# Prompt attention of a hybrid decoder step: scores from 64-row halves with strided queries, mask added in PSUM, a new order of the turns

## The chip, the cores and the metric

The kernel runs on one core of one Trainium2 chip, as one launch. The metric is the device time of the launch in microseconds (us), the median of several runs. A measurement of this kernel can tell a difference of about 0.2% (6.5 us) from none.

## What is computed

One inference step of one decoder layer, for a prompt of 1024 tokens and 32 sample tokens (8 sequences of 4) with shared weights, model width 1024. Per layer: RMS norm, one input projection, an RWKV-7 branch (16 heads of 64), a dilated sliding-window attention branch, gates and an output projection, a squared-ReLU MLP, a gated embedding, and a final norm. The change touches only the attention of the prompt:

```python
def dilated_attn_prompt(q, k, v, dilation, n_back):
    ...
    qb = to_blocks(q)
    kb = with_prev(to_blocks(k))
    vb = with_prev(to_blocks(v))
    s = jnp.einsum('ndbqhe,ndbkhe->ndbhqk', qb, kb) * ATTN_SCALE
    ...
    s = jnp.where(mask[None, None, :, None], s, NEG)
    m = jnp.max(s, axis=-1, keepdims=True)
    e = jnp.exp(s - m)
    den = jnp.sum(e, axis=-1, keepdims=True)
    o = jnp.einsum('ndbhqk,ndbkhe->ndbqhe', e / den, vb)
    lse = (m + jnp.log(den))[..., 0].transpose(0, 1, 2, 4, 3)
```

There are three groups of four heads with head width 64. Their windows and dilations are (128, 1), (512, 4) and (2048, 16). Everything is float32.

## The kernel before, in words

The program goes through its stages one after another; each is a block in which the five engines run their own instruction lists and meet at its end. For each group g of 0, 1, 2 there are three blocks: the projection of q, k and v (`attention_projection`), the prompt's attention (`attention_prompt`), and the scores of the sample tokens (`sample_scores`). Then `attention_ends` reads back what the prompt's attention has stored in DRAM and weights the groups. The RWKV pairs, the merge, the MLP and the rest follow.

`qT` and `kT` hold queries and keys with features on the partitions: two heads share a tile of 128 rows, head 0 in rows 0 to 63 and head 1 in rows 64 to 127. `attention_prompt` takes 8 turns per group, one per 128 queries. A turn has 128 or 256 keys: in group 0 256 from turn 1 on, in group 1 128 in even turns and 256 in odd ones, in group 2 always 128. In groups 1 and 2 the tokens of a turn lie 4 and 8 elements apart in `qT` and `kT`.

A turn t of the kernel before is this:

- GpSimd copies the queries of each head into its row half of `qz` (L419). VectorE has set `qz` to zero at the block's start (L467), so the other half of each 128-row stationary operand is zero.
- TensorE multiplies them with the keys, four matmuls into the PSUM tile `S[t % 2]` (L440). S has two buffers.
- VectorE adds the mask and writes the result to `sc` in SBUF (L474), then takes the negated maximum per row into `stage` (L477). `stage` has two buffers.
- ScalarE takes four exponentials, one per head, with the row sums as a second output, into `ex` (L496).
- TensorE transposes `ex` into PSUM `PT` (L449), ScalarE copies it to `pt` (L498), TensorE multiplies with the values into PSUM `O` (L457).
- VectorE copies O into `stage` (L481) and SyncE stores `stage` to `attention_rows` in DRAM (L514).

The order on each engine is written out: on TensorE `scores(t+1)`, then `rest(t)` (transposes and values of t); on VectorE `maxima(t+1)` (mask and maximum), then `values(t)` (the copy of O); on ScalarE the four exponentials of t, then the copy of t. The maximum of turn t waits for the landed store of turn t-2, which read the same half of `stage`:

```python
vec.wait_ge(stored[s], (k + g * (NB // 2)) * 16)
vec_s.done("max", nc.vector.tensor_reduce(stage[:, s, AW:AW + HPG], ...
```

At the start of each `attention_prompt` ScalarE also issues the prefetch DMAs for later blocks (L489). The turns run in hardware loops of two turns (`turns` and `turns_ahead`, loops at L364, L369 and L383), with register arithmetic for addresses and semaphore values.

Of the kernel before, what the change touches and what calls it, by code (L numbers as in the profile page):

```python
# [17 lines left out]
P = 128  # L18
# [313 lines left out]
def prompt_counts(nc, top):  # L332

    sem = lambda n: top.enter_context(nc.semaphore(f"att_{n}"))
    names = {"pool": ["q0", "q1"], "score": ["scores"], "pe": ["pt", "pv"], "vec": ["mask", "max"], "out": ["o"], "act": ["e0", "e1", "e2", "e3", "pt"]}
    return [Steps(sem(n), names[n], ahead=2) for n in names], sem("zero"), [sem(f"stored{s}") for s in range(2)]


def attention_prompt(nc, top, g, counts, psum, qT, kT, vtok, att, ident, scratch, prefetch):

    with ExitStack() as ctx:
        sb = lambda n, *s: ctx.enter_context(nc.sbuf_tensor(f"{n}{g}", [P, *s], F32))
        qz, stage = sb("qz", 2, 2, 2, BL), sb("stage", 2, STG)
        sc, ex, pt = sb("sc", HPG, 2 * BL), sb("ex", HPG, 2 * BL), sb("pt", HPG, 2, BL)
# [3 lines left out]
        (pool_s, score_s, pe_s, vec_s, out_s, act_s), zero, stored = counts  # L351
# [3 lines left out]
        def turns(eng, unit):  # L355

            def run(t, half_t, parity):
                first = half_t if g == 1 else t
                both = {0: not (isinstance(t, int) and t == 0), 1: parity == 1, 2: False}[g]
                unit(t, first, both, parity, half_t)  # L360

            if g == 0:
                run(0, 0, 0)
                with eng.Fori(0, NB // 2 - 1) as i:  # L364
                    run(2 * i + 1, i, 1)
                    run(2 * i + 2, i + 1, 0)
                run(NB - 1, NB // 2 - 1, 1)
            else:
                with eng.Fori(0, NB // 2) as i:  # L369
                    run(2 * i, i, 0)  # L370
                    run(2 * i + 1, i, 1)

        def turns_ahead(eng, first_part, rest):

            def run(part, t, half_t, parity):
                both = {0: not (isinstance(t, int) and t == 0), 1: parity == 1, 2: False}[g]
                part(t, half_t if g == 1 else t, both, parity, half_t)

            run(first_part, 0, 0, 0)
            if g == 0:  # L380
                run(first_part, 1, 0, 1)
                run(rest, 0, 0, 0)
                with eng.Fori(0, NB // 2 - 1) as i:  # L383
                    run(first_part, 2 * i + 2, i + 1, 0)
                    run(rest, 2 * i + 1, i, 1)
                    run(first_part, 2 * i + 3, i + 1, 1)
                    run(rest, 2 * i + 2, i + 1, 0)
            else:
                with eng.Fori(0, NB // 2 - 1) as i:
                    run(first_part, 2 * i + 1, i, 1)  # L390
                    run(rest, 2 * i, i, 0)
                    run(first_part, 2 * i + 2, i + 1, 0)
                    run(rest, 2 * i + 1, i, 1)
                run(first_part, NB - 1, NB // 2 - 1, 1)
                run(rest, NB - 2, NB // 2 - 1, 0)
            run(rest, NB - 1, NB // 2 - 1, 1)

        with nc.Block() as block:
            @block.gpsimd
            def _(pool):  # L400
                if g == 0:
                    pool_s.begin(pool)
                pool.wait_ge(zero, g + 1)

                def unit(t, f, both, s, k):
                    score_s.wait(pool, "scores", t - 2)
                    for h in range(2):
                        rows = slice(h * HD, (h + 1) * HD)
                        src = qT[rows, :, 0:SEQ]
                        if g == 0:  # L410
                            src = src[:, :, bass.ds(f * BL, BL)]
                            dst = qz[rows, s, :, h, :]
                        elif g == 1:
                            src = src.rearrange("p a (i r) -> p a r i", r=STEP[1])[:, :, bass.ds(f, 1), (BL if both else 0):(2 * BL if both else BL)].rearrange("p a o i -> p a (o i)")
                            dst = qz[rows, s, :, h, :]
                        else:
                            src = src.rearrange("p a (i r) -> p a r i", r=STEP[2])[:, :, bass.ds(f, 1), :].rearrange("p a o i -> p a (o i)")
                            dst = qz[rows, s, :, h, :]
                        pool_s.done(f"q{h}", nc.gpsimd.tensor_copy(dst, src))  # L419
                turns(pool, unit)  # L420

            @block.tensor
            def _(pe):
                if g == 0:
                    pe_s.begin(pe)
                if g == 0:
                    score_s.begin(pe)

                def scores(t, f, both, s, k):
                    nk = 2 * BL if both else BL  # L430
                    pool_s.wait(pe, "q1", t)
                    vec_s.wait(pe, "mask", t - 2)
                    for h in range(HPG):
                        if g == 0:
                            keys = dilated(kT[:, h // 2, 0:SEQ], 0, f - 1 if both else f, nk)
                        elif g == 1:
                            keys = dilated(kT[:, h // 2, 0:SEQ], 1, f, nk, 0)
                        else:
                            keys = dilated(kT[:, h // 2, 0:SEQ], 2, f, nk)
                        last = nc.tensor.matmul(S[s][:, h, 0:nk], qz[:, s, h // 2, h % 2, :], keys, start=True, stop=True)  # L440
                    score_s.done("scores", last)

                def rest(t, f, both, s, k):
                    nk = 2 * BL if both else BL
                    act_s.wait(pe, "e3", t)
                    act_s.wait(pe, "pt", t - 1)
                    for h in range(HPG):
                        for b in range(nk // BL):
                            last = nc.tensor.transpose(PT[:, h, b, :], ex[:, h, b * BL:(b + 1) * BL], ident)  # L449
                    pe_s.done("pt", last)  # L450
                    act_s.wait(pe, "pt", t)
                    out_s.wait(pe, "o", t - 1)
                    for h in range(HPG):
                        for b in range(nk // BL):
                            blk = (t - 1 + b) if both else t
                            v = vtok[:, bass.ds(blk, 1), h * HD:(h + 1) * HD].rearrange("p o c -> p (o c)")
                            last = nc.tensor.matmul(O[:, h * HD:(h + 1) * HD], pt[:, h, b, :], v, start=b == 0, stop=b == nk // BL - 1)  # L457
                    pe_s.done("pv", last)
                turns_ahead(pe, scores, rest)

            @block.vector
            def _(vec):
                if g == 0:
                    vec_s.begin(vec)
                if g == 0:
                    out_s.begin(vec)
                nc.vector.memset(qz[:, :, :, :, :], 0.0).then_inc(zero, 1)  # L467

                def maxima(t, f, both, s, k):
                    nk = 2 * BL if both else BL  # L470
# [6 lines left out]
                    vec_s.done("max", nc.vector.tensor_reduce(stage[:, s, AW:AW + HPG], sc[:, :, 0:nk], AXX, ALU.max, negate=True))  # L477

                def values(t, f, both, s, k):
                    pe_s.wait(vec, "pv", t)  # L480
                    out_s.done("o", nc.vector.tensor_copy(stage[:, s, 0:AW], O))  # L481
                turns_ahead(vec, maxima, values)

            @block.scalar
            def _(act):
                if g == 0:
                    act_s.begin(act)
                for dst, src, loaded in prefetch:
                    act.dma_start(dst, src).then_inc(loaded, 16)  # L489

                def unit(t, f, both, s, k):
                    nk = 2 * BL if both else BL
                    vec_s.wait(act, "max", t)
                    pe_s.wait(act, "pt", t - 1)
                    for h in range(HPG):
                        act_s.done(f"e{h}", nc.scalar.activation(ex[:, h, 0:nk], sc[:, h, 0:nk], ACT.Exp, bias=stage[:, s, AW + h:AW + h + 1], accum_out=stage[:, s, AW + HPG + h:AW + HPG + h + 1]))  # L496
                    pe_s.wait(act, "pt", t)
# [1923 lines left out]
```

## Time and profile before

| | |
|---|---|
| median of 3 runs | 3240.7 us (3236.83 to 3241.89) |
| the profiled execution: its own time | 3243.15 us |
| its span | 3241.3 us |
| PE (TensorE) busy | 2892.0 us, 89% of the span |
| DVE (VectorE) busy | 1093.4 us, 34% |
| ACT (ScalarE) busy | 954.7 us, 29% |
| POOL (GpSimd) busy | 408.0 us, 13% |
| the three prompt-attention blocks | about 145 to 209, 313 to 387 and 491 to 550 us of the span |

PE is the matrix engine's matmuls, PEld its weight loads, SPq and ACTq the queues that issue DMAs. A float32 matmul appears as two records. PEclk is the granted TensorE clock as a share of 2.4 GHz; 0.50 means 1.2 GHz all the time.

### The profile page before, as it was taken

The page shows a single profiled execution, that of the slowest core. Times are in us where ns is not written, and L with a number is a line of the kernel's source. Part 1 is how long each engine was busy: PE and PEld are TensorE (multiplying, and loading weights), DVE is VectorE, ACT ScalarE, POOL GpSimd, SP SyncE. Part 2 cuts the span into 40 slices and gives each one's busy share as a digit, 9 for nine tenths or more (in the row PEclk, how much of TensorE's full clock was granted, in tenths as well). Part 3 has the DMA queues.
Part 4 walks back from the last instruction along what each step waited for, and adds up shares of the span by engine and source line. Part 5 has one row for each costly group of instructions (what it writes and reads, how often), then busy time and mean ns, then how long its engine had stood idle before and what let it go on. Part 6 is the DMA issues. An engine that isn't in the chain of part 4 may idle for free. (4 is left out here: it accounts for less than half of the span.)

```text
span 3241.3 us, 62579 instructions
## 1 busy us (share of the span) xinstructions
PE 2892.0 (89%) x27170; PEld 2307.8 (71%) x27170; DVE 1093.4 (34%) x2436; ACT 954.7 (29%) x1797; POOL 408.0 (13%) x398
## 2 busy tenths in 40 slices
PE   5888795699999999999978999898999999999797
PEld 3666575356666666666665666597999999999685
DVE  1120202247777777777760101103111111111222
ACT  1120202145555555555541000003122211122212
POOL 0000001011111111211100000011121212121010
PEclk8989796799999999999978999999999999999898
DMA  3211104200100100101001001111111111111011
GB/s 138 80 64 60 71 14 148 65 22 3 34 25 11 34 19 17 34 3 33 13 2 69 29 34 42 39 66 39 39 45 39 45 39 39 45 39 45 30 41 62
DMA packets 57762, 139.16 MB, mean 43 GB/s; under 512 B 5041, under 2 KB 37041, under 8 KB 52433
## 3 DMA queue, kind: packets, MB, share of 16 engines
q1 hardware_dynamic: 53376, 112.89, 10.3%
q10 hardware_dynamic: 4176, 23.20, 2.1%
q8 instruction: 166, 2.72, 0.3%
q14 instruction: 44, 0.35, 0.0%
HBM read 119.54 MB, written 16.54 MB: 42 GB/s over the span
## 5 line engine op out<-in xcount | busy, mean ns | idle before, releaser
L1557 PE MATMUL psum<-hT,rkv_w 128*64 128x256 f32 (+1 forms) x3072 | 411.9, 395 | 11.5 <-DMA rkv_w<-in_w_pair 10.2
L1557 PEld LDWEIGHTS psum<-hT,rkv_w 128*64 128x64 f32 x3072 | 212.6, 138 | 116.0 <-issue 31.4
L129 PE MATMUL psum<-hT,merge_w 128*128 128x352 f32 x768 | 232.4, 463 | 12.1 <-DMA merge_w<-in_w_mix 12.1
L1878 POOL TENSOR_TENSOR ff_w_low<-ff_raw,ff_w_high 128x1024 fp32r<-128x1024 f32 x64 | 157.3, 2457 | 677.8 <-ACT ff_w_high L1873 677.8
L129 PEld LDWEIGHTS psum<-hT,merge_w 128*128 128x128 f32 x768 | 147.1, 192 | 95.2 <-issue 15.0
L152 PE MATMUL psum<-ff_high,ff_w_high 128*128 128x352 f32 x768 | 173.2, 335 | 38.7 <-DVE ff_low L2177 38.7
L2180 DVE TENSOR_TENSOR rwkv_out<-rwkv_out,psum 128x1056 f32<-128x1056 f32 x64 | 80.3, 1254 | 321.1 <-PE psum L152 321.1
L152 PE MATMUL psum<-h_high,ff_w_high 128*128 128x352 f32 x768 | 167.6, 326 | 13.0 <-DVE h_low L226 12.6
L152 PE MATMUL psum<-ff_low,ff_w_high 128*128 128x352 f32 x768 | 170.3, 331 | 0.0
L152 PE MATMUL psum<-ff_high,ff_w_low 128*128 128x352 f32 x768 | 169.9, 330 | 0.0
L1873 ACT ACTIVATE ff_w_high<-ff_raw 128x1024 fp32r<-128x1024 f32 x64 | 67.3, 1052 | 347.5 <-PE psum L152 347.5
L152 PE MATMUL psum<-h_low,ff_w_high 128*128 128x352 f32 x768 | 166.2, 325 | 0.0
L152 PE MATMUL psum<-h_high,ff_w_low 128*128 128x352 f32 x768 | 166.2, 324 | 0.0
L152 PEld LDWEIGHTS psum<-ff_high,ff_w_high 128*128 128x128 f32 x768 | 136.0, 197 | 41.0 <-issue 41.0
L2177 DVE TENSOR_TENSOR ff_low<-ff_up,ff_high 128x1056 fp32r<-128x1056 f32 x32 | 40.3, 1258 | 351.4 <-ACT ff_high L2162 351.4
L129 PE MATMUL psum<-hT,w_qk 128*128 128x352 f32 x432 | 130.9, 466 | 22.6 <-DMA w_qk<-in_w_qk 21.3
L152 PEld LDWEIGHTS psum<-h_high,ff_w_high 128*128 128x128 f32 x768 | 131.3, 190 | 15.0 <-issue 10.8
L152 PEld LDWEIGHTS psum<-ff_high,ff_w_low 128*128 128x128 f32 x768 | 135.9, 194 | 0.0
L152 PEld LDWEIGHTS psum<-ff_low,ff_w_high 128*128 128x128 f32 x768 | 135.5, 195 | 0.0
L1997 DVE TENSOR_TENSOR merge_prod<-merge_gate,psum 128x1056 f32<-128x1056 f32 x16 | 20.1, 1255 | 335.7 <-PE psum L129 335.7
L129 PEld LDWEIGHTS psum<-hT,w_qk 128*128 128x128 f32 x432 | 83.1, 193 | 69.9 <-DMA w_qk<-in_w_qk 21.8
L152 PEld LDWEIGHTS psum<-h_high,ff_w_low 128*128 128x128 f32 x768 | 132.6, 189 | 0.0
(323 smaller groups left out, 5209.0 us busy)
## 6 DMA issues: line engine op xcount, KB each, us to landing
ff_raw<-in_w_ff SPq DMA_DIRECT2D x64, 512.0 KB, 3.5
merge_w<-in_w_mix SPq DMA_DIRECT2D x8, 1664.0 KB, 6.9
rkv_w<-in_w_pair SPq DMA_DIRECT2D x24, 512.0 KB, 4.1
rwkv_out<-in_kc ACTq DMA_DIRECT2D x4, 2048.0 KB, 13.1
ple_w<-in_w_ple SPq DMA_DIRECT2D x8, 640.0 KB, 3.9
x_in<-in_xT SPq DMA_DIRECT2D x2, 2112.0 KB, 11.1
rwkv_out<-in_xT ACTq DMA_DIRECT2D x1, 4224.0 KB, 14.1
out_yT<-y SPq DMA_DIRECT2D x8, 528.0 KB, 3.1
```

What stands on the lines that cost most here:

```text
L129: last = nc.tensor.matmul(acc[:, n, 0:TT], w[:, k, :], x[:, k, n * TT:(n + 1) * TT], start=k == 0, stop=k == kt - 1)
L152: last = nc.tensor.matmul(acc[:, n, 0:TT], a[:, k, :], b[:, k, n * TT:(n + 1) * TT], start=k == 0 and b is x_hi and a is w_hi, stop=k == k ...
L1557: mm = nc.tensor.matmul(ahead[half[a], 0:width(v)], w3[:, k, n * P + a * C:n * P + a * C + C], hT[:, k, cols(v)], start=k == 0, stop=k == ...
L1873: return nc.scalar.activation(parts[0][:, s, :], raw[:, s, 0:KT * P], ACT.Copy)
L1878: return nc.gpsimd.tensor_tensor(parts[1][:, s, :], raw[:, s, 0:KT * P], parts[0][:, s, :].bitcast(F32), ALU.subtract)
L1997: vec_s.done(f"mul{b}", nc.vector.tensor_tensor(thirds(prod[:, b, :]), thirds(gate[:, b if nb == 2 else s, :]), acc[1][:, :, 0:TT], ALU.mult))
L2177: vec_s.done(f"low{c}", nc.vector.tensor_tensor(ff[1][:, c, :], up[:, c % 2, :], ff[0][:, c, :].bitcast(F32), ALU.subtract))
L2180: vec_s.done(f"add{m}", nc.vector.tensor_tensor(thirds(x[:, m, :]), thirds(x[:, m, :]), acc[m % 2][:, :, 0:TT], ALU.add))
```

## The change

Queries are no longer copied: each head's scores are a matmul over its own 64 rows of `qT` and `kT`, with the stationary queries read in place (strided in groups 1 and 2). The four heads' scores are placed so that the heads of the upper and the lower row half write different PSUM banks (`slot`). `qz`, its memset, GpSimd's copies and `sc` are gone. The mask is added to S in place, in PSUM, and the maximum and the exponentials read PSUM. `ex` has two buffers. TensorE takes the scores of turn t+2 between the transposes and the values of turn t. ScalarE copies turn t-1's transposes between the second and the third exponential of turn t. The copy has a semaphore of its own. All turns are written out, without hardware loops.

```diff
-    names = {"pool": ["q0", "q1"], "score": ["scores"], "pe": ["pt", "pv"], "vec": ["mask", "max"], "out": ["o"], "act": ["e0", "e1", "e2", "e3", "pt"]}
+    names = {"score": ["scores"], "pe": ["pt", "pv"], "vec": ["mask", "max"], "out": ["o"], "act": ["e0", "e1", "e2", "e3"], "copy": ["pt"]}
...
-        qz, stage = sb("qz", 2, 2, 2, BL), sb("stage", 2, STG)
-        sc, ex, pt = sb("sc", HPG, 2 * BL), sb("ex", HPG, 2 * BL), sb("pt", HPG, 2, BL)
+        stage = sb("stage", 2, STG)
+        ex, pt = sb("ex", 2, HPG, 2 * BL), sb("pt", HPG, 2, BL)
...
+        slot = lambda h: 2 * (h % 2) + h // 2
+        both = lambda t: (t > 0, t % 2 == 1, False)[g]
+        keyed = lambda t: 2 * BL if both(t) else BL
...
+                def scores(t):
+                    act_s.wait(pe, "e3", t - 2)
+                    for b in range(2):
+                        for a in range(2):
+                            rows = slice(a * HD, (a + 1) * HD)
+                            last = nc.tensor.matmul(S[t % 2][:, slot(2 * b + a), 0:keyed(t)], queries(t, rows, b), keys(t, rows, b), start=True, stop=True)
+                    score_s.done("scores", last)
+
+                def turned(t):
+                    act_s.wait(pe, "e3", t)
+                    copy_s.wait(pe, "pt", t - 1)
...
+                def values(t):
+                    copy_s.wait(pe, "pt", t)
+                    out_s.wait(pe, "o", t - 1)
...
+                for t in range(2):
+                    scores(t)
+                for t in range(NB):
+                    turned(t)
+                    if t + 2 < NB:
+                        scores(t + 2)
+                    values(t)
...
-                nc.vector.memset(qz[:, :, :, :, :], 0.0).then_inc(zero, 1)
...
+                def maxima(t):
+                    s, nk = t % 2, keyed(t)
                     m = att("pairs") if g == 2 else att("band")[:, 2 * BL - nk:]
                     score_s.wait(vec, "scores", t)
-                    act_s.wait(vec, "e3", t - 1)
-                    vec_s.done("mask", nc.vector.tensor_tensor(sc[:, :, 0:nk], S[s][:, :, 0:nk], m[:, None, :].to_broadcast([P, HPG, nk]), ALU.add))
+                    vec_s.done("mask", nc.vector.tensor_tensor(S[s][:, :, 0:nk], S[s][:, :, 0:nk], m[:, None, :].to_broadcast([P, HPG, nk]), ALU.add))
                     vec_s.wait(vec, "mask", t)
-                    vec.wait_ge(stored[s], (k + g * (NB // 2)) * 16)
+                    vec.wait_ge(stored[s], (t // 2 + g * (NB // 2)) * 16)
...
+                maxima(0)
+                for t in range(NB):
+                    if t + 1 < NB:
+                        maxima(t + 1)
+                    values(t)
...
+                for t in range(NB):
                     vec_s.wait(act, "max", t)
-                    pe_s.wait(act, "pt", t - 1)
-                    for h in range(HPG):
-                        act_s.done(f"e{h}", nc.scalar.activation(ex[:, h, 0:nk], sc[:, h, 0:nk], ACT.Exp, bias=stage[:, s, AW + h:AW + h + 1], accum_out=stage[:, s, AW + HPG + h:AW + HPG + h + 1]))
-                    pe_s.wait(act, "pt", t)
-                    act_s.done("pt", nc.scalar.activation(pt[:, :, 0:nk // BL, :], PT[:, :, 0:nk // BL, :], ACT.Copy))
-                turns(act, unit)
+                    pe_s.wait(act, "pt", t - 2)
+                    for h in (0, 1):
+                        weights(t, h)
+                    if t:
+                        copied(t - 1)
+                    for h in (2, 3):
+                        weights(t, h)
+                copied(NB - 1)
```

`weights(t, h)` is the exponential of head h, and `copied(t)` the copy of turn t's transposes, which waits for the transposes of t and the values of t-1.

ScalarE in group 0, one loop body of two turns of the kernel before (`ex` is written by the exponentials, `pt` by the copy; L117 rows are waits and register arithmetic):

```order
L496 ACTIVATE ex,stage<-sc,stage 128x256 [waits att_pe]
L496 ACTIVATE ex,stage<-sc,stage 128x256 x3
L117 REGISTER_ALU
L498 ACTIVATE pt<-psum 128x1024 [waits att_pe]
L117 ISA
L496 ACTIVATE ex,stage<-sc,stage 128x256 [waits att_pe,att_vec]
L496 ACTIVATE ex,stage<-sc,stage 128x256 x3
L117 REGISTER_ALU
L498 ACTIVATE pt<-psum 128x1024 [waits att_pe]
```

The same place in the changed kernel, from the first turn on (L446 is the exponential, L451 the copy):

```order
L446 ACTIVATE ex,stage<-psum,stage 128x128 [waits att_pe,att_vec]
L446 ACTIVATE ex,stage<-psum,stage 128x128 x3
L446 ACTIVATE ex,stage<-psum,stage 128x256 [waits att_pe,att_vec]
L446 ACTIVATE ex,stage<-psum,stage 128x256
L451 ACTIVATE pt<-psum 128x4x128 [waits att_pe]
L446 ACTIVATE ex,stage<-psum,stage 128x256 x2
L446 ACTIVATE ex,stage<-psum,stage 128x256 [waits att_pe,att_vec]
L446 ACTIVATE ex,stage<-psum,stage 128x256
L451 ACTIVATE pt<-psum 128x1024 [waits att_pe]
L446 ACTIVATE ex,stage<-psum,stage 128x256 x2
```

The copy of a turn has moved behind the first two exponentials of the next turn.

TensorE in the changed kernel, group 0, turns 0 and 1 (L390 transposes, L382 scores, L400 values):

```order
L390 MATMUL psum<-cst_sb,ex 128x128 [waits att_copy,att_act]
L390 MATMUL psum<-cst_sb,ex 128x128 x3
L382 MATMUL psum<-kT,qT 128x256 [waits att_act]
L382 MATMUL psum<-kT,qT 128x256 x3
L400 MATMUL psum<-vtok,pt 128x64 [waits att_out,att_copy]
L400 MATMUL psum<-vtok,pt 128x64 x3
L390 MATMUL psum<-cst_sb,ex 128x128 [waits att_copy,att_act]
L390 MATMUL psum<-cst_sb,ex 128x128 x7
L382 MATMUL psum<-kT,qT 128x256 [waits att_act]
L382 MATMUL psum<-kT,qT 128x256 x3
L400 MATMUL psum<-vtok,pt 128x64 [waits att_out,att_copy]
L400 MATMUL psum<-vtok,pt 128x64 x7
```

Scores stand between transposes and values; before, they stood ahead of the transposes, and the values followed the transposes with only a wait between.

VectorE in the changed kernel, group 0, from turn 1's mask on (L421 mask, L424 maxima, L428 the copy of O):

```order
L421 TENSOR_TENSOR psum<-psum,att_sb 128x1024 [waits att_score]
L424 TENSOR_REDUCE stage<-psum 128x2x2 [waits att_stored1,att_vec]
L428 COPY stage<-psum 128x256 [waits att_pe]
L421 TENSOR_TENSOR psum<-psum,att_sb 128x1024 [waits att_score]
L424 TENSOR_REDUCE stage<-psum 128x2x2 [waits att_stored0,att_vec]
L428 COPY stage<-psum 128x256 [waits att_pe]
```

The order of the three is that of the kernel before. The mask no longer waits for the exponentials (att_act), since it writes no `sc`.

## Rows read from the trace of the kernel before

**Rows 1.** Busy times by stretch: from:to, us, each engine busy (instructions), clock, DMA share, GB/s
```profile
145.00:209.00 64.00, 48.02 (x244) 41.22 (x244) 22.91 (x26) 23.94 (x72) 6.48 (x17) 0.74 0.23 83
...
313.00:387.00 74.00, 49.07 (x208) 39.75 (x208) 19.32 (x25) 21.15 (x72) 10.14 (x16) 0.66 0.34 114
...
491.00:550.00 59.00, 37.03 (x160) 32.74 (x160) 15.33 (x25) 17.84 (x72) 10.23 (x16) 0.59 0.43 143
```

**Rows 2.** Timeline, group 0, one turn: start us, us, engine, instruction [idle before <-releaser]
```profile
171.57 1.95 PE L440 MATMUL psum<-kT,qz 128*128 x8
...
173.35 1.04 PE L449 MATMUL psum<-cst_sb,ex 128*128 128x128 f32 x8
173.67 1.22 DVE L474 TENSOR_TENSOR sc<-psum,att_sb 128x1024 f32<-128x1024 f32 x1 [1.47 <-PE psum L440]
...
174.43 1.02 ACT L498 ACTIVATE pt<-psum 128x1024 f32<-128x1024 f32 x1 [1.99 <-PE psum L449]
175.03 1.22 DVE L477 TENSOR_REDUCE stage<-sc 128x4 f32<-128x1024 f32 x1
...
175.69 1.99 PE L457 MATMUL psum<-vtok,pt 128*128 x16 [1.30 <-ACT pt L498]
176.28 0.51 ACT L496 ACTIVATE ex<-sc,stage 128x256 f32<-128x256 f32 x1 [0.83 <-DVE stage L477]
...
177.52 3.41 PE L440 MATMUL psum<-kT,qz 128*128 x8
...
177.72 0.42 DVE L481 COPY stage<-psum 128x256 f32<-128x256 f32 x1 [1.47 <-PE psum L457]
```

**Rows 3.** Timeline, the last turn of group 0
```profile
199.38 1.97 PE L449 MATMUL psum<-cst_sb,ex 128*128 128x128 f32 x8 [0.53 <-ACT ex L496]
...
202.46 3.67 PE L457 MATMUL psum<-vtok,pt 128*128 128x64 f32 x16 [1.11 <-ACT pt L498]
206.17 0.42 DVE L481 COPY stage<-psum 128x256 f32<-128x256 f32 x1 [6.86 <-PE psum L457]
```

**Rows 4.** Timeline, first and last copies of O, delayed maxima, values at 128 keys
```profile
155.98 0.42 DVE L481 COPY stage<-psum 128x256 f32<-128x256 f32 x1
...
160.03 1.22 DVE L477 TENSOR_REDUCE stage<-sc 128x4 f32<-128x1024 f32 x1 [0.71 <-DMA attention_rows<-stage]
...
333.10 0.42 DVE L481 COPY stage<-psum 128x256 f32<-128x256 f32 x1 [1.51 <-PE psum L457]
...
338.08 0.69 DVE L477 TENSOR_REDUCE stage<-sc 128x4 f32<-128x512 f32 x1 [2.28 <-DMA attention_rows<-stage]
...
384.07 0.42 DVE L481 COPY stage<-psum 128x256 f32<-128x256 f32 x1 [8.62 <-PE psum L457]
...
511.70 0.42 DVE L481 COPY stage<-psum 128x256 f32<-128x256 f32 x1 [2.58 <-PE psum L457]
...
516.60 0.69 DVE L477 TENSOR_REDUCE stage<-sc 128x4 f32<-128x512 f32 x1 [2.15 <-DMA attention_rows<-stage]
...
537.39 1.10 PE L457 MATMUL psum<-vtok,pt 128*128 x8 [0.87 <-ACT pt L498]
...
541.93 1.97 PE L457 MATMUL psum<-vtok,pt 128*128 128x64 f32 x8 [0.69 <-ACT pt L498]
...
547.44 0.42 DVE L481 COPY stage<-psum 128x256 f32<-128x256 f32 x1 [3.08 <-PE psum L457]
```

**Rows 5.** The 24 stores of stage to DRAM (L514), from issue to landing
```profile
DMA to landing us min/median/max: 1.7/1.7/4.3
```

**Rows 6.** Timeline, the first exponential of group 1; then all 24 copies of L498
```profile
327.33 0.40 ACT L496 ACTIVATE ex<-sc,stage 128x128 f32<-128x128 f32 x1 [51.38 <-issue]
...
L498 ACT ACTIVATE pt<-psum x24: 597/598/1025, 154.2 to 544.8; 128x512 f32<-128x512 f32 x13, 128x1024 f32<-128x1024 f32 x11
```

**Rows 7.** Timeline, the start of group 0: VectorE's memset and TensorE's first scores
```profile
145.98 0.91 DVE L467 MEMSET qz<- 128x1024 f32 x1 [4.75 <-ACTq L109]
...
147.85 2.50 PE L440 MATMUL psum<-kT,qz 128*128 128x128 f32 x9 [7.07 <-POOL qz L419]
```

More of the change, by code:

```diff
@@ L350, in attention_prompt @@
         O = psum[:, 6, 0:AW]
-        (pool_s, score_s, pe_s, vec_s, out_s, act_s), zero, stored = counts
+        (score_s, pe_s, vec_s, out_s, act_s, copy_s), stored = counts
         for each in counts[0]:
             each.first = g * NB
[L355 to L396, printed above, removed]
@@ L398, in attention_prompt @@
-        with nc.Block() as block:
[L399 to L420, printed above, removed]
@@ L425, in _ @@
                     pe_s.begin(pe)
-                if g == 0:
                     score_s.begin(pe)
[L429 to L432, printed above, removed]
-                    for h in range(HPG):
[L434 to L441, printed above, removed]
@@ L459, in _, with queries, keys @@
-                turns_ahead(pe, scores, rest)
+                def queries(t, rows, b):
+                    if g == 0:
+                        return qT[rows, b, t * BL:(t + 1) * BL]
+                    lo = BL if g == 1 and both(t) else 0
+                    return qT[rows, b, 0:SEQ].rearrange("p (i r) -> p r i", r=STEP[g])[:, first(t), lo:lo + BL]
+                def keys(t, rows, b):
+                    if g == 0:
+                        lo = t * BL - (BL if both(t) else 0)
+                        return kT[rows, b, lo:lo + keyed(t)]
+                    return kT[rows, b, 0:SEQ].rearrange("p (i r) -> p r i", r=STEP[g])[:, first(t), 0:keyed(t)]
@@ new lines, in scores @@
+                def scores(t):
[8 more added lines that the diff above has]
+                    copy_s.wait(pe, "pt", t - 1)
+                    for h in range(HPG):
+                        for b in range(keyed(t) // BL):
+                            last = nc.tensor.transpose(PT[:, h, b, :], ex[:, t % 2, h, b * BL:(b + 1) * BL], ident)
+                    pe_s.done("pt", last)
@@ new lines, in values @@
+                def values(t):
+                    copy_s.wait(pe, "pt", t)
+                    out_s.wait(pe, "o", t - 1)
+                    blocks = keyed(t) // BL
+                    for h in range(HPG):
+                        for b in range(blocks):
+                            v = vtok[:, t - blocks + 1 + b, h * HD:(h + 1) * HD]
+                            last = nc.tensor.matmul(O[:, h * HD:(h + 1) * HD], pt[:, h, b, :], v, start=b == 0, stop=b == blocks - 1)
+                    pe_s.done("pv", last)
@@ L503, in _ @@
                 rows = scratch.rearrange("(i r) c -> r i c", r=STEP[g])
-                def unit(t, f, both, s, k):
+                for t in range(NB):
                     out_s.wait(sp, "o", t)
@@ L508, in unit @@
                     if g == 0:
-                        dst = scratch[bass.ds(f * BL, BL), g * STG:(g + 1) * STG]
-                    elif g == 1:
-                        dst = rows[bass.ds(f, 1), (BL if both else 0):(2 * BL if both else BL), g * STG:(g + 1) * STG].rearrange("o i c -> (o i) c")
-                    else:
-                        dst = rows[bass.ds(f, 1), :, g * STG:(g + 1) * STG].rearrange("o i c -> (o i) c")
-                    sp.dma_start(dst, stage[:, s, :]).then_inc(stored[s], 16)
-                turns(sp, unit)
+                        dst = scratch[t * BL:(t + 1) * BL, g * STG:(g + 1) * STG]
+                    else:
+                        lo = BL if g == 1 and both(t) else 0
+                        dst = rows[first(t), lo:lo + BL, g * STG:(g + 1) * STG]
+                    sp.dma_start(dst, stage[:, t % 2, :]).then_inc(stored[t % 2], 16)
                 for s in range(2):
```

37 lines of the change are left out of this document (13 added, 24 removed).

## The prediction

> **What bounds the kernel now.** I read the stretches first, then the timeline of one turn, then who waits for whom. The change touches only the three prompt-attention blocks, about 64, 74 and 59 us of the 3241.3 us span [rows 1]; the rest keeps its instructions. TensorE is busy 75, 66 and 63% of them, at a granted clock of 0.74, 0.66 and 0.59. Between the levels 1.2 and 2.4 GHz that is 52, 68 and 82% of the time at 1.2.
>
> A turn's loop closes on TensorE [rows 2]: scores of the next turn 1.95, transposes 1.04, then the wait for ScalarE's copy of 1.02 us, values 1.99, and the next scores at 177.52, 5.95 us after the last ones. The mask, the maxima and the four exponentials run beside it. At 1.2 GHz the next scores take 3.41 us, and a group's last turn has transposes of 1.97 and values of 3.67 [rows 2, 3]. So the first group takes 50.19 us from its first to its last copy of O (155.98 to 206.17), 7.17 a turn; the second 50.97 (333.10 to 384.07), the third 35.74 (511.70 to 547.44) [rows 3, 4]. These seven intervals per group are what I recompute.
>
> One more dependence hardly shows yet. The maxima of turn t+2 go into the stage buffer that the store of turn t reads, so they wait until that store has landed, 1.7 us (median) after its issue [rows 5]. VectorE waits there only for the first store of each group (0.71, 2.28 and 2.15 us [rows 4]), when the prefetches load the DMA engines: from the end of the O copy to the start of the maxima 3.6, 4.6 and 4.5 us. Elsewhere the new scores come later than the store.
>
> **The change, part by part.**
> *The order on ScalarE decides.* Before, the copy of turn t comes ahead of the exponentials of t+1. Now it comes behind the first two of them. VectorE's order stays: maxima of t+1, O copy of t, maxima of t+2. This closes a loop with one turn per round: O copy (t) → store lands → maxima (t+2) → two exponentials (t+2) → copy of the transposes (t+1) → values (t+1) → O copy (t+1). In the kernel before, the same path runs through all four exponentials, the transposes and the copy of its own turn: two turns per round, about 10.5 us, hence covered by TensorE's loop. "Two turns ahead" doesn't help: VectorE won't touch those scores before the O copy.
>
> The round for 256 keys, from rows: store 1.85 (1.7 plus the hops), maxima 1.22, hop 0.1, two exponentials and the accumulator read 1.08, copy 1.02, hop 0.07, values 1.99, hop 0.05, O copy 0.42 [rows 2, 5]: **7.8 us with values at 2.4 GHz, 9.5 at 1.2** (3.67) [rows 3]. The mask (0.04 + 1.22) lies under the store's 1.85. For 128 keys maxima take 0.69, an exponential 0.40, the copy 0.60, values 1.10 or 1.97 [rows 4, 6]: 5.75 or 6.6. The second group alternates 128 and 256 keys: rounds of 7.06 and 6.49 at 2.4, of 8.74 and 7.36 at 1.2.
>
> *Clock.* TensorE's work per round shrinks or stays while the round grows, so I expect no less time at 1.2 GHz than now: 60, 75 and 90% in the three groups against 52, 68 and 82. Rounds: 8.8; 8.3 and 7.1; 6.5.
>
> *Sum per group*, six rounds, the late first store, and a last turn (transposes, copy, values in a row: 199.38 to 206.17 = 6.8 [rows 3]; third group 1.0 + 0.6 + 1.97 + hops = 3.8):
> first 52.8 + 1.8 + 6.8 = 61.4 against 50.2: +11.2;
> second 46.2 + 2.7 + 6.8 = 55.7 against 51.0: +4.7;
> third 39.0 + 2.6 + 3.8 = 45.4 against 35.7: +9.7.
>
> *Start.* The memset and the first query copies go: scores could begin at 145.98 instead of 147.85 in the first group [rows 7]. But the first copy of O now also waits for the maxima of turn 1. I take -1, between -1.9 and 0. In the other groups ScalarE first issues its own prefetch DMAs, and the first exponential of the second group starts only at 327.33, and what ended the idle time before it is "issue", not the maxima [rows 6]. This stays, so nothing is gained there.
>
> *Scores in row halves, strided queries.* No row shows these forms. They stand outside the new loop: per round TensorE has values, transposes and scores, at 1.2 GHz with full-price scores 3.67 + 1.97 + 3.41 = 9.05, under 9.5 [rows 2, 3]. Whether halves overlap (half the price) or strided weights cost as much again only inside that slack changes nothing: 0, with an upper bound of about +1 a round in the first group, +6. The Trainium skill, page "TensorEngine Tiling (Array Packing)", section "Theoretical Speedup", gives up to 2x for a contraction of 64 rows; by that rule alone the time would fall (rival 1). No run here shows row halves of this form.
>
> *No copies on GpSimd:* off the path after the start, 0. *Loops written out:* register instructions ahead of values go. TensorE's idle time ahead of values is 1.30 us in the written loop (copy 1.02) and 1.11 in the last turn outside it [rows 2, 3]; my hop of 0.07 has it.
>
> *Mask and maxima in PSUM.* The mask from PSUM into SBUF takes 1.22, the maxima from SBUF also 1.22 for 1024 elements [rows 2]; place makes no difference in these rows, so 0. Upper bound: maxima twice as dear, +1.2 in some 18 rounds, up to +22, which I think far. The Trainium skill ("Perfetto Trace Analysis", section "Optimizing Scalar/DVE Operations") puts an access at about 60 ns for VectorE in SBUF and 125 in PSUM, for ScalarE 93 and 51. By it, as an estimate, each round's maxima gain 0.065 and two exponentials lose 0.084: -0.4 us in all, against 0 by the rows.
>
> **Sum:** 11.2 + 4.7 + 9.7 - 1 = **+24.6 us**. The profiled execution took 3243.15 us, 1.85 more than its span, so it would take 3267.7. It lies 2.45 above the median of 3240.7; on the median's scale the forecast is **3265.3**.
>
> **Rivals.**
> 1. *TensorE's loop remains the bound (faster).* If the O copy did not hold back the next maxima, scores would fill the wait for ScalarE's copy (1.2 us a turn) and cost half (1.35 saved at mixed clocks): -2.5 a turn in the first group, -1.9 and -1.5 in the others, times 7: -41, 3200. For it: TensorE is the busiest engine, and every removed part is its work or ahead of it. Against: the written order on VectorE and ScalarE is fixed. It decides if stores and maxima need under 1 us together; rows say 1.85 + 1.22. 8%.
> 2. *Clock at 2.4 throughout.* Rounds of 7.8; 7.06 and 6.49; 5.75 give +5.2, -0.8, +5.2, less 1: +8.6, 3249. Against: the blocks before spend over half at 1.2 with denser work. With mixed cases near no change: 10%.
> 3. *Clock at 1.2 throughout.* +15.4, +6.8, +10.4, less 1: +31.6, 3272. Part of the forecast's range.
> 4. *PSUM or late stores dearer.* Maxima from PSUM or a second late store per group add 5 to 22: 3270 to 3294, of which over 3281 about 10%.
> 5. *The halves don't overlap:* hidden, the same time; not a case of its own.
>
> **How the numbers follow.** Forecast with its clock and store bounds (3250 to 3281) 72%, rival 1 8%, rival 2 10%, rival 4 beyond the range 10%. Over 0.2% (6.5 us, about what a measurement can tell) is under 3234 or over 3247. Faster 0.08, same 0.08 (the low part of rival 2 and mixed cases), slower 0.84. The range, 3246 to 3281, takes rival 2's end and leaves out rival 1 and the far part of 4.
>
> **What would show it.** Right: VectorE's maxima wait for the DMA attention_rows in nearly all turns with a predecessor (18 rather than 3), O copies 7.8 to 9.5 us apart in the first group and 5.7 to 6.6 in the third, TensorE idle for 2 to 4 us ahead of the values, waiting on ScalarE's copy; blocks of some 74, 79 and 68 us. The scores end several us before their mask starts. Wrong: O copies under 7 us apart in the first group; masks that wait on scores; a shorter block anywhere but in the second group; or a difference outside the three blocks.

## The result, and the profile after

The changed kernel takes 3270.23 us (median of 4 runs, 3266.95 to 3272.05), the one before 3238.76 us in the same comparison: a ratio of 1.0098, 95% interval 1.0083 to 1.0113, about 1% slower. The profiled executions are 3243.15 us before and 3270.32 after, spans 3241.3 and 3268.5: +27.2. The forecast was +24.6 us and 3265.3, range 3246 to 3281. In this text "the changed kernel" is the one with the whole change, "the kernel before" the one without it.

Busy times by stretch after (from:to, length, then PE, PEld, DVE, ACT, POOL busy with instructions, granted clock, DMA share, GB/s), over the three prompt-attention blocks:

```profile
145.00:222.00 77.00, 52.69 (x244) 44.31 (x244) 21.65 (x25) 22.00 (x72) 0.24 (x2) 0.57 0.19 69
326.00:402.00 76.00, 42.09 (x208) 34.61 (x208) 18.35 (x25) 19.45 (x72) 0.15 (x1) 0.57 0.33 111
508.00:574.00 66.00, 32.22 (x160) 27.26 (x158) 13.87 (x24) 16.04 (x72) 0.00 (x0) 0.50 0.38 128
```

Against [rows 1] GpSimd's work is gone and the blocks are longer. In the second and third group TensorE has less busy time than before, yet its clock is lower in all three: 0.57, 0.57 and 0.50 instead of 0.74, 0.66 and 0.59. At 0.50 the whole third block ran at 1.2 GHz.

The timeline after: one round of group 0, from one copy of O to the next; then the first and last copies of O of each group and, in group 1, two inner ones (start, length, engine, instruction, idle before and its releaser):

```profile
154.72 0.42 DVE L428 COPY stage<-psum 128x256 f32<-128x256 f32 x1 [3.88 <-PE psum L400]
...
177.05 1.92 PE L390 MATMUL psum<-cst_sb,ex 128*128 128x128 f32 x8
177.30 0.42 DVE L428 COPY stage<-psum 128x256 f32<-128x256 f32 x1 [5.74 <-PE psum L400]
177.64 1.22 DVE L421 TENSOR_TENSOR psum<-psum,att_sb 128x1024 f32<-128x1024 f32 x1
178.90 2.08 PE L382 MATMUL psum<-kT,qT 64*128 64x256 f32 x8
179.59 1.22 DVE L424 TENSOR_REDUCE stage<-psum 128x4 f32<-128x1024 f32 x1 [0.73 <-DMA attention_rows<-stage]
180.85 0.47 ACT L446 ACTIVATE ex<-psum,stage 128x256 f32<-128x256 f32 x1 [6.41 <-DVE stage L424]
...
181.77 1.02 ACT L451 ACTIVATE pt<-psum 128x1024 f32<-128x1024 f32 x1
...
182.84 2.21 PE L400 MATMUL psum<-vtok,pt 128*128 128x64 f32 x16 [1.86 <-ACT pt L451]
...
185.09 0.42 DVE L428 COPY stage<-psum 128x256 f32<-128x256 f32 x1 [4.27 <-PE psum L400]
...
219.10 0.42 DVE L428 COPY stage<-psum 128x256 f32<-128x256 f32 x1 [6.07 <-PE psum L400]
...
346.39 0.42 DVE L428 COPY stage<-psum 128x256 f32<-128x256 f32 x1 [14.29 <-PE psum L400]
...
364.89 0.42 DVE L428 COPY stage<-psum 128x256 f32<-128x256 f32 x1 [3.60 <-PE psum L400]
...
371.72 0.42 DVE L428 COPY stage<-psum 128x256 f32<-128x256 f32 x1 [3.84 <-PE psum L400]
...
399.21 0.42 DVE L428 COPY stage<-psum 128x256 f32<-128x256 f32 x1 [6.07 <-PE psum L400]
...
527.52 0.42 DVE L428 COPY stage<-psum 128x256 f32<-128x256 f32 x1 [15.77 <-PE psum L400]
...
571.90 0.42 DVE L428 COPY stage<-psum 128x256 f32<-128x256 f32 x1 [3.08 <-PE psum L400]
```

Read the round as a chain. The copy of O ends at 177.72 and its store lands; the maxima start at 179.59, 1.87 us later. They release the exponentials at 180.85; behind two of these stands ScalarE's copy at 181.77, behind it the values at 182.84, behind them the next copy of O at 185.09. A round of 7.79 us, with its values nearly all at 2.4 GHz (2.21 us; 1.99 and 3.67 at the two levels [rows 2, 3]). The mask and the scores run inside it without setting anything. It is the shortest full round of the group: its seven intervals between copies of O are 11.75, 10.83, 7.79, 8.62, 9.24, 9.66 and 6.49 us. The first two have a late store, and in four of the first six the values take 3.67 or 3.68 us, which is 1.2 GHz.

From first to last copy of O the groups take 64.38, 52.82 and 44.38 us against 50.19, 50.97 and 35.74 [rows 3, 4]: +24.7 of the 27.2 us. The first copy of O comes 1.3 us earlier than before, the stretches between the groups are 1.0 us longer, and the stretch behind the last copy of O is 2.7 us longer. That last difference lies in code that the change leaves alone, and can't be told from scatter: in the thirteen profiled executions of this study the stretch takes between 2690.1 and 2697.6 us, whatever the order of the turns.

The maxima after, what ended VectorE's idle time ahead of them, and who waited for them:

```profile
L424 DVE TENSOR_REDUCE stage<-psum x24: 691/692/1226, 147.4 to 564.3; 128x4 f32<-128x512 f32 x13, 128x4 f32<-128x1024 f32 x11
its engine sat idle before it (us, times) until:
  DMA attention_rows<-stage: 27.8, 18
who waited for it (us, times):
  ACT ex L446: 243.7, 22
```

Eighteen waits for the store instead of three, and an unchanged duration in PSUM (at most 1.226 us for 1024 elements; 1.22 in [rows 2]).

### The profile page after: what moved, and what is told of

The parts are those of the page before. It is cut to its first block and busy times, and to the rows that moved or that the text cites. A ratio compares the mean times of both kernels' runs of the same rounds, so it can differ in the third digit from the quotient of the medians.

```text
span 3268.5 us, 61980 instructions
## 1 busy us (share of the span) xinstructions
PE 2888.5 (88%) x27170; PEld 2303.5 (70%) x27170; DVE 1089.8 (33%) x2433; ACT 948.9 (29%) x1797; POOL 380.9 (12%) x350
```

## The experiments

**1. The orders and the store, one at a time.** Three kernels start from the changed one. `copy_back` puts ScalarE's copy ahead of the next turn's exponentials:

```diff
-                    for h in (0, 1):
-                        weights(t, h)
-                    if t:
-                        copied(t - 1)
-                    for h in (2, 3):
+                    for h in range(HPG):
                         weights(t, h)
-                copied(NB - 1)
+                    copied(t)
```

`four_stages` gives `stage` four buffers with a semaphore each (the exponentials, the copy of O and the store use `t % 4` too):

```diff
-        stage = sb("stage", 2, STG)
+        stage = sb("stage", 4, STG)
...
-                    vec.wait_ge(stored[s], (t // 2 + g * (NB // 2)) * 16)
+                    vec.wait_ge(stored[t % 4], (t // 4 + g * (NB // 4)) * 16)
```

`both` has the two together. What was expected:

> The changed kernel with ScalarE's copy of a turn back ahead of the next turn's exponentials. Theory (the one-turn loop through store, maxima, two exponentials, copy and values sets the rounds): without the moved copy the loop spans two turns again, rounds fall to 5.2 to 7.7 us at 256 keys and about 4.3 at 128, and the kernel takes about 3215 us, some 55 less than the changed kernel and about 25 less than the one before. Rival (the mask in PSUM, the strided queries or the written-out code cost the time): it stays within 10 us of the changed kernel, 3260 or more.

> The changed kernel with four stage buffers instead of two, so that maxima no longer wait for the store of two turns before; orders as changed. Theory: the store's share of the loop goes (27.8 us of VectorE's waits for the DMA in the changed kernel), the maxima follow the mask at once, the O copy still holds back the mask: about 3243 us, the level of the kernel before. Rival (the stores hide behind the O copy and the mask anyway, the order alone costs): under 8 us gained, 3262 or more.

> Copy back and four stage buffers together. Theory: the two loops are alternatives once the copy is back, so the second repair adds only the late first stores, 2 to 3 us per group: about 3208 us. Rival (the two add up): 55 and 27 less than the changed kernel, about 3188 us.

Measured: copy_back 3227.43 us, ratio to the kernel before 0.9963 (0.9949 to 0.9977); four_stages 3235.74, 0.9987 (0.9978 to 0.9997); both 3208.25, 0.9902 (0.9885 to 0.9918). Against the changed kernel's 3270.23 that is 43, 34 and 62 us less.

The moved copy is the largest part, as forecast, though with it back the time fell less than the 55 us expected. The loop through the store spans two turns now and still binds in part: in `copy_back` the maxima still wait for the DMA, and taking that wait away as well (`both`) gains 19 us more. Idle time of VectorE and ScalarE ahead of what reads or writes `stage`:

```profile
  issue: 103.5, 2
  PE psum L400: 90.6, 19
  DVE stage L424: 64.7, 14
  DMA attention_rows<-stage: 28.2, 18
```

So my "two alternatives" were wrong: the second repair is worth 19 us behind the first, not 2 to 3 per group. They don't add up to 77 either; together they gain 62. `four_stages` alone gained 34 us where 27 were expected. In it no maxima wait for the DMA, and the round's path has mask and maxima back to back:

```profile
170.42 0.42 DVE L428 COPY stage<-psum 128x256 f32<-128x256 f32 x1 [5.73 <-PE psum L400]
170.76 1.22 DVE L421 TENSOR_TENSOR psum<-psum,att_sb 128x1024 f32<-128x1024 f32 x1
172.02 1.23 DVE L424 TENSOR_REDUCE stage<-psum 128x4 f32<-128x1024 f32 x1
173.28 0.47 ACT L446 ACTIVATE ex<-psum,stage 128x256 f32<-128x256 f32 x1 [5.71 <-DVE stage L424]
```

The maxima start 1.18 us after the copy of O ends, instead of 1.87. The round from 170.42 to the next copy of O at 177.30 takes 6.88 us instead of 7.79 and still has the moved copy and the values in it. From first to last copy of O group 0 takes 50.17 us instead of 64.38; besides the shorter round, the late stores no longer count there, and the granted clock of its block is 0.67 instead of 0.57.

**2. The moved copy alone, in the kernel before.** `copy_moved` leaves everything as before except ScalarE's order (its turns written out, the copy with a semaphore of its own):

```diff
-                    for h in range(HPG):
-                        act_s.done(f"e{h}", ...)
-                    pe_s.wait(act, "pt", t)
-                    act_s.done("pt", ...)
+                    for h in (0, 1):
+                        weights(t, h)
+                    if t:
+                        copied(t - 1)
+                    for h in (2, 3):
+                        weights(t, h)
```

> The kernel before with one thing of the change: ScalarE copies turn t-1 between the second and third exponential of turn t (its turns written out, the other engines' loops kept). Theory: the loop closes here too, and longer, since the next scores stand behind the values on TensorE: scores 1.95 to 3.41, mask and maxima 2.5, two exponentials 1.1, copy 1.0, values 2.0 to 3.7 = 8.8 to 12 us a round at 256 keys and 5.3 to 7.3 at 128, about 50 us more than before, 3290 us. Rival (the order is harmless, the PSUM operands or row halves cost): within 7 us of the kernel before.

(The cut diff leaves out the two helpers, which are those of the changed kernel on `sc`, and the renamed semaphore.) Measured: 3296.09 us, 1.0178 (1.0161 to 1.0195), 6 us from the forecast. One round of its group 0:

```profile
191.76 3.73 PE L440 MATMUL psum<-kT,qz 128*128 x8
192.00 0.42 DVE L481 COPY stage<-psum 128x256 f32<-128x256 f32 x1 [5.88 <-PE psum L457]
...
195.62 1.23 DVE L474 TENSOR_TENSOR sc<-psum,att_sb 128x1024 f32<-128x1024 f32 x1 [3.19 <-PE psum L440]
196.88 1.22 DVE L477 TENSOR_REDUCE stage<-sc 128x4 f32<-128x1024 f32 x1
198.14 0.51 ACT L496 ACTIVATE ex<-sc,stage 128x256 f32<-128x256 f32 x1 [9.00 <-DVE stage L477]
...
199.13 1.00 ACT L502 ACTIVATE pt<-psum 128x1024 f32<-128x1024 f32 x1
...
200.19 3.67 PE L457 MATMUL psum<-vtok,pt 128*128 x16 [3.27 <-ACT pt L502]
...
203.90 0.42 DVE L481 COPY stage<-psum 128x256 f32<-128x256 f32 x1 [5.79 <-PE psum L457]
```

Every piece of the loop is in line, 11.9 us per turn. It closes through another engine than in the changed kernel: the scores of the next turn but one stand behind the values on TensorE, and the mask waits for them (3.19 us idle), not for a store. Nothing of PSUM, row halves or strides is in this kernel: ScalarE's order, written out, costs 56 us here.

**3. Is the copy's new place bad in itself?** `moved_copy_free_maxima` keeps the changed kernel's copy where it is and opens the loop elsewhere, with four stage buffers and VectorE's maxima of t+2 ahead of the copy of O of t. `maxima_free` is the same with the copy back.

```diff
                 maxima(0)
+                maxima(1)
                 for t in range(NB):
-                    if t + 1 < NB:
-                        maxima(t + 1)
+                    if t + 2 < NB:
+                        maxima(t + 2)
                     values(t)
```

> Copy back, four stage buffers, and on VectorE the mask and maxima of t+2 ahead of the O copy of t. Theory: the O copy no longer holds back the maxima, so truly two turns ahead; only the loop of exponentials, scores, mask and maxima over two turns and TensorE's own work remain: 4.0 to 4.5 us a turn at 2.4 GHz, 5 to 10 us less than with the first two repairs, about 3201 us. Rival (the delayed O copy holds up the values of the next turn): the same 3208 or more.

> The changed kernel with its moved copy kept, four stage buffers, and the maxima of t+2 ahead of the O copy of t. Theory: the moved copy costs only because it closes a loop through the O copy; with the maxima free of the O copy that loop is open, and the kernel is within 8 us of the one with the copy back (3192 us). Rival (the copy between the exponentials costs by itself, by delaying the values): 3215 us or more.

Measured: maxima_free 3191.82 us, 0.9846 (0.9830 to 0.9862); moved_copy_free_maxima 3194.39, 0.9856 (0.9839 to 0.9872). The two overlap. The fair comparison has four stage buffers on both sides: there the place of the copy is worth 27 us with the maxima held (`four_stages` 3235.74, `both` 3208.25) and nothing that can be measured with the maxima free. With two buffers and the maxima held it is 43 us. So the cost is the closed loop, not the copy between exponentials. `maxima_free` gained 16 us over `both`, more than the 5 to 10 expected.

**4. What the other parts are worth.** `old_orders` has both orders of the kernel before (copy back; TensorE's scores of t+1 ahead of the transposes of t) on the changed kernel's row halves, strided queries, PSUM mask and written-out turns, with two stage buffers.

```diff
-                for t in range(2):
-                    scores(t)
-                for t in range(NB):
-                    turned(t)
-                    if t + 2 < NB:
-                        scores(t + 2)
-                    values(t)
+                scores(0)
+                for t in range(NB):
+                    if t + 1 < NB:
+                        scores(t + 1)
+                    turned(t)
+                    values(t)
```

> The changed kernel with both orders as before: ScalarE copies a turn ahead of the next exponentials, TensorE takes the scores of t+1 ahead of the transposes of t. What is left of the change are the row halves, the mask in PSUM, the missing copies and the written-out turns. Theory: these parts are a gain once the one-turn loop is gone; the scores are on TensorE's loop again, at 1.1 to 2.1 us instead of 1.95 to 3.4, so 1 to 1.4 us less per turn of 256 keys and half of it at 128: about 3213 us. Rival (these parts cost): above the kernel before, 3245 or more.

Measured: 3234.75 us, 0.9978 (0.9966 to 0.9989). A gain, 7 us, but a quarter of what I expected. The scores did get cheaper: in group 0 the eight records of 64x256 take 2.08 us at 1.2 GHz, where those of 128*128 take 3.73 at that clock (first line of the `copy_moved` round above; the 3.41 in [rows 2] were measured at a granted clock of 0.55, partly above 1.2 GHz). But the clock went down with the work. Stretches of old_orders over the three blocks:

```profile
143.00:206.00 63.00, 45.59 (x244) 36.68 (x244) 22.56 (x25) 22.30 (x72) 0.68 (x2) 0.67 0.26 93
308.00:381.00 73.00, 47.69 (x208) 38.95 (x208) 18.87 (x25) 19.89 (x72) 0.11 (x1) 0.50 0.36 120
486.00:544.00 58.00, 33.86 (x160) 28.07 (x160) 14.35 (x25) 16.59 (x72) 0.13 (x1) 0.50 0.43 146
```

Clock 0.67, 0.50 and 0.50 against 0.74, 0.66 and 0.59 in [rows 1]: groups 1 and 2 now run wholly at 1.2 GHz. The third group shows what that costs. Its inner turns last 4.95 to 4.96 us in old_orders, each with values at 1.2 GHz (1.97 us). In the kernel before, the turns with values at 1.2 GHz (1.96 us) last 5.4 to 5.9 us, and the two with values at 2.4 GHz (1.10 us) 4.64 and 4.79. So at the same clock a turn became 0.5 to 1.0 us shorter, and the lost turns at 2.4 GHz took part of that back. Besides, the maxima wait 14.2 us for the stores here, against 5.1 before. No run holds the clock fixed, so how the missing 21 us divide between the two is not shown.

`scores_twice` issues each score matmul of the changed kernel twice (`for b in (0, 1, 0, 1)`), the second time over the same result.

> The changed kernel with the four score matmuls of each turn issued twice. Theory: the scores lie outside the loop, TensorE idles longer ahead of the values than they take; between -3 and +4 us against the changed kernel, 3267 to 3274 (less is possible only through a higher granted clock). Rival (row-half scores are on the path): 1.3 to 2.1 us more in each of 24 turns, about +40 us, 3310.

Measured: 3260.88 us, ratio to before 1.0058 (1.0041 to 1.0075), 9 us less than the changed kernel although TensorE does more, and below the 3267 to 3274 that I expected. Its stretches:

```profile
143.00:216.00 73.00, 50.02 (x308) 43.34 (x308) 21.84 (x25) 22.04 (x72) 0.43 (x2) 0.73 0.20 73
320.00:398.00 78.00, 50.76 (x272) 41.43 (x272) 18.35 (x25) 19.48 (x72) 0.15 (x1) 0.68 0.33 109
504.00:568.00 64.00, 37.81 (x218) 33.02 (x216) 13.97 (x24) 16.07 (x72) 0.00 (x0) 0.55 0.40 132
```

The clock is 0.73, 0.68 and 0.55 where the changed kernel has 0.57, 0.57 and 0.50. The scores are off the path, as claimed: with twice as many the rival's 3310 is 49 us away. And TensorE's idle time is not free here, since less of it came with a higher clock for the values, which are on the path: group 0 takes 58.70 us from first to last copy of O instead of 64.38. The 9 us are not all explained by this. Group 1 takes 2.0 us more and group 2 1.8 less, so that only 5.8 of the profiled executions' 12.3 us lie ahead of the last copy of O. The rest lies behind it, in the stretch that varies by as much from kernel to kernel (2690.1 to 2697.6 us, as above).

**5. Towards a faster kernel.** In every kernel of this study so far the first exponentials of groups 1 and 2 wait for ScalarE's own DMA issues. The start of group 1 in `both`, ScalarE's timeline:

```profile
291.93 6.50 ACTq L442 DMA_DIRECT2D rwkv_out<-in_kc  x2
298.46 7.00 ACTq L442 DMA_DIRECT2D w_qk<-in_w_qk  x1
305.49 0.45 ACTq L442 DMA_DIRECT2D w_kv<-in_w_kv  x1
306.05 0.37 ACT L446 ACTIVATE ex<-psum,stage 128x128 f32<-128x128 f32 x1 [51.41 <-issue]
```

The issue of the first 1.5 MB of weights took 7 us with two 2 MB transfers issued just ahead of it. In group 0, where those two have 0.5 MB each, it took 1.63. Why an issue takes so long is not shown: the next one, of another 1.5 MB and with more ahead of it, took 0.45. The same place in `prefetch_spread` (below), where one transfer is issued and nothing else:

```profile
290.03 0.70 ACTq L455 DMA_DIRECT2D rwkv_out<-in_kc  x1
292.86 0.37 ACT L445 ACTIVATE ex<-psum,stage 128x128 f32<-128x128 f32 x1 [40.13 <-DVE stage L424]
```

`prefetch_spread` is `both` with the issues ahead of turns 0, 2, 4 and 5:

```diff
-                for dst, src, loaded in prefetch:
-                    act.dma_start(dst, src).then_inc(loaded, 16)
+                issued = {0: 0, 2: 1, 4: 2, 5: 3}
...
                 for t in range(NB):
+                    if t in issued:
+                        dst, src, loaded = prefetch[issued[t]]
+                        act.dma_start(dst, src).then_inc(loaded, 16)
```

`all_repairs` adds VectorE's order of maxima_free. `all_scores_twice` is all_repairs with doubled scores.

> Copy back and four stage buffers, and ScalarE issues its four prefetch DMAs one by one, ahead of the exponentials of turns 0, 2, 4 and 5, instead of all at the block's start. Theory: the first exponentials of groups 1 and 2 wait 13 to 14 us for the second and third issue, which stall behind the first transfer; spread, the issues cost 0.5 us each and about 24 us go: 3184 us. Rival (an issue of these descriptors takes 6 to 7 us wherever it stands, or the data come too late for the sample scores and the next weights): no gain, 3208 or more.

> Copy back, four stage buffers, maxima ahead of the O copy, prefetches spread. Theory: the last two gains (16 and 27 us) lie in different places, the turns and the wait for the first exponential, and add up: about 3165 us. Rival (without the wait at the start the prefetches run into the turns, TensorE is slower there): 3175 or more.

> The kernel with all repairs and every score matmul issued twice. Theory (TensorE's work beyond the loop raises the granted clock, as in the run before, where doubled scores made the changed kernel 9 us faster): in groups 1 and 2, which run at 1.2 GHz, the clock rises, and the time is the same or up to 8 us less than with the repairs alone. Rival (with short turns TensorE is the bound, the scores are on its path): 0.7 to 2.1 us more a turn, 15 to 40 us more.

Measured: prefetch_spread 3181.03 us, 0.9817 (0.9800 to 0.9833), 27 less than `both`; all its issues take 0.33 to 0.70 us. all_repairs **3173.16 us**, 0.9797 (0.9780 to 0.9813): the best of the study, 68 us under the kernel before in its own comparison (3241.29) and 97 under the changed one. It missed its 3165 by 8: the free maxima are worth 8 us there, not 16. all_scores_twice 3182.79, 0.9822 (0.9806 to 0.9839): 10 us more. The clock rises here too, but now the scores are on the path: in group 1 the masks wait for them 25.9 us in 8 waits, against 17.6 in 8 in all_repairs. Neither of my two sizes was right, and the expectation took group 1 to run at 1.2 GHz, where all_repairs has 0.75. The higher clock may give back a part of the added work; it does not give back all.

Stretches of groups 1 and 2 in all_repairs:

```profile
285.00:335.00 50.00, 36.01 (x208) 29.04 (x208) 20.17 (x26) 19.56 (x72) 1.52 (x2) 0.75 0.59 190
430.00:480.00 50.00, 36.30 (x185) 29.64 (x188) 17.82 (x28) 16.15 (x72) 1.52 (x2) 0.56 0.57 190
```

The same in all_scores_twice: clock 0.93 and 0.78 instead of 0.75 and 0.56, with 6.7 and 5.4 us more of busy TensorE.

```profile
285.00:335.00 50.00, 42.71 (x268) 32.99 (x266) 18.20 (x24) 18.88 (x72) 0.00 (x0) 0.93 0.58 188
430.00:480.00 50.00, 41.71 (x255) 36.22 (x255) 14.98 (x26) 14.82 (x67) 0.00 (x0) 0.78 0.55 182
```

## Why the prediction was right

*The loop.* The step "the order on ScalarE decides" held in every link: 18 waits for the DMA, values waiting on the copy (122.5 us of TensorE's idle time), and a chain in which every piece follows the one before. The one full round with values near 2.4 GHz took 7.79 us where 7.8 was computed, the two wholly at 1.2 GHz behind the late stores 9.24 and 9.66 where 9.5 was. Runs 1 to 3 show it from three sides: undoing the copy's place, putting it into the old kernel, and opening the loop at another point.

*The sum per group* was +11.2, +4.7 and +9.7; measured +14.2, +1.9 and +8.6. That 24.7 before the start's gain came so near to 25.6 is partly luck, errors of opposite sign. Group 0: I took 60% of the time at 1.2 GHz, and at a granted clock of 0.57 it was 86%; and the first store held the maxima 4.4 us behind the copy of O instead of 3.6, the second 3.5 instead of 1.85. Group 1: I took three quarters of the values at 1.2 GHz, but a round from 364.89 to 371.72 takes 6.83 us, which only values of 256 keys at 2.4 GHz allow (7.06 by my sum). Group 2: all at 1.2 GHz, and 1.0 us under my sum over seven intervals, with exponentials a little shorter than I took them. The blocks, forecast at 74, 79 and 68 us, are about 77, 76 and 66.

*The start.* The first copy of O in group 0 comes at 154.72 instead of 155.98; about 0.9 us of that is the block's own, the rest its earlier begin. Forecast: -1.

*Mask and maxima in PSUM:* priced at 0, measured 1.22 us for the maxima as before. By the Trainium skill's page "Perfetto Trace Analysis", section "Optimizing Scalar/DVE Operations", they would, as an estimate, have been 0.065 us longer each; the maxima went from 1.22 us [rows 2] to 1.226 at most, so this trace does not show it. The other half of that estimate, exponentials 0.042 us shorter each, the trace does bear out: 0.47 us from PSUM for 256 elements against 0.51 from SBUF [rows 2].

*Row halves:* priced at 0 for the changed kernel because hidden. scores_twice shows that they are. The reading behind the upper bound was slightly off: scores at 1.2 GHz cost 3.73 us, not 3.41, so that values, transposes and full-price scores take 9.37 us, still under 9.5. What the halves save is now seen too: 2.08 against 3.73 us at 1.2 GHz, short of the factor of two that the Trainium skill's page "TensorEngine Tiling (Array Packing)", section "Theoretical Speedup", gives as an upper limit.

*Strided queries* were left at 0 as well, and the changed kernel hides them too. The faster kernels show their price. The scores of a turn of 256 keys in all_repairs, first in group 0, where queries and keys lie side by side, then in group 1, where they lie 4 elements apart, both at a granted clock of 1.00:

```profile
154.40 1.13 PE L382 MATMUL psum<-kT,qT 64*128 64x256 f32 x8
...
306.90 2.19 PE L382 MATMUL psum<-kT,qT 64*128 64x256 f32 x8
```

At 1.2 GHz the same two forms take 2.08 and 2.19 us (old_orders), so with the stride the higher clock gains nothing. Two things add up. The keys' stride, which the kernel before has too: a matmul record of 256 keys takes 634 ns (median) instead of 376 (for 128 keys 408 in the kernel before and 410 in all_repairs, so the queries' stride adds nothing there). And the queries' stride, which is new: a weight load takes 307 to 326 ns instead of 186, where the kernel before, with queries copied side by side, had 208 in group 1 at 2.4 GHz. The halves still pay: the scores of 128 keys in group 1 take 1.30 us in all_repairs and 2.02 in the kernel before, both at 2.4 GHz.

*The rivals.* Rival 1 (TensorE's loop remains the bound) hung on the condition that the copy of O does not hold back the next maxima. The changed kernel doesn't meet it. moved_copy_free_maxima does, with four stage buffers, and took 3194.39 us, 47 less than the kernel before, where the rival computed 41. For the parts without the orders the gain was 7 us: the rival's price for the cheaper scores took the clock as fixed. Rival 3, the clock at 1.2 GHz throughout, gives 3272, nearer to the measured 3270.23 than the forecast of 3265.3 is; but groups 0 and 1 were not wholly at 1.2 GHz (0.57), and group 0's second late store, which rival 4 had priced, added time that rival 3 lacks. The +27.2 us of the profiled pair is 2.6 more than forecast; the comparison's medians differ by 31.5, and the interval of the ratio (+27 to +37 us) takes in the former.

## What to carry to other kernels

With engines that run written orders, draw each engine's order of two turns side by side and look for a chain that comes back to its start one turn later: its length is the time per turn, however idle every engine is. Work that stands ahead ("two turns ahead") helps only if every engine on the way may start it ahead; here VectorE's in-order copy of O and the two stage buffers held it. Before moving an instruction behind another engine's result, ask what that result itself waits for.

## What the runs showed of the hardware that I had not expected

With less TensorE work in old_orders the granted clock was lower (0.74, 0.66, 0.59 before; 0.67, 0.50, 0.50 with it), and the kernel gained 7 us instead of about 28. Useless extra matmuls beside the critical loop came with a higher clock (0.57, 0.57, 0.50 to 0.73, 0.68, 0.55) and a kernel 9 us faster, of which 5.8 us can be seen in the turns. In the fastest kernel, where the scores are on the path, the same extra matmuls raised the clock too and cost 10 us. The four score matmuls of a turn with strided operands took 2.19 us at 2.4 GHz as at 1.2. A DMA issue on ScalarE took 7.00 us behind two 2 MB transfers on the same queue, the issue right after it 0.45, and one with none ahead of it 0.70.
